# Down-projection one pair later in a software-pipelined mixture-of-experts loop

## What is computed

```
g_sel    = argmax(h @ w_group)                 # one of 8 groups
top_idx  = top_k(e_logits in the group, 2)     # two of its 8 experts
y        = (silu(xb @ w1[e]) * (xb @ w3[e])) @ w2[e]      # for each expert e, xb its tokens
out[tok] += gate * y
```

## Time and profile before

| | |
|---|---|
| median of 3 runs | 1690.52 us |
| lowest, highest | 1689.78, 1690.87 us |
| profiled execution, its own time | 1692.09 us |
| its span in the profile | 1689.8 us |
| mean granted TensorE clock | 0.911 of full speed |
| PE busy | 1341.6 us, 79% |
| DVE, ACT, POOL busy | 480.5, 287.4, 321.6 us |
| read from HBM | 453.15 MB |

### The profile page before, as it was taken

One profiled execution on the slowest core, in us unless ns is written; L12 is line 12 of the kernel. 1 busy time (PEld: TensorE's weight loads), 2 busy tenths in 40 slices (PEclk: granted clock), 3 DMA queues, 4 the chain that ended last, 5 costly groups with the idle time before them and its releaser, 6 DMA issues.

```text
span 1689.8 us, 19504 instructions
## 1 busy us (share of the span) xinstructions
PE 1341.6 (79%) x6100; PEld 630.5 (37%) x6100; DVE 480.5 (28%) x904; ACT 287.4 (17%) x562; POOL 321.6 (19%) x439
## 2 busy tenths in 40 slices
PE   6988984988877878785689699956988787888872
PEld 4555452333332323232444376443333232333330
DVE  6996124111111111111407653142111111111112
ACT  3335110110000001010243433111110000001000
POOL 6303001232222221211000000002232222222210
PEclk9999986999999989998789799977999999999996
DMA  5105541999999999995220302264999999999984
GB/s 204 50 1 219 218 164 62 396 384 406 403 398 403 401 405 410 398 393 218 70 106 1 112 1 103 97 276 169 392 399 399 396 404 398 407 409 395 400 348 178
DMA packets 82068, 464.31 MB, mean 275 GB/s; under 512 B 13457, under 2 KB 15681, under 8 KB 32481
## 3 DMA queue, kind: packets, MB, share of 16 engines
q1 hardware_dynamic: 68640, 436.86, 65.6%
q0 software_dynamic: 11648, 20.47, 3.7%
q10 hardware_dynamic: 1728, 6.29, 0.9%
HBM read 453.15 MB, written 18.94 MB: 279 GB/s over the span
## 4 chain that ended last, share of the span: by engine, by line
PE 41%; SPq 30%; DVE 12%; issue 7%; DMA 6%; ACT 3%; POOLq 0%; POOL 0%; DVEq 0%; ACTq 0%
SPq L1506 20%; PE ps L1368 13%; SPq L1511 10%; PE ps L1388 6%; DMA ring<-in_moe_w 4%; PE ps L442 3%; PE ps L873 2%; PE ps L316 2%; PE ps L431 2%; PE ps L391 2%; DVE ring L541 1%; DMA region_a<-ytok 1%; PE ps L926 1%; DVE extra L541 1%; PE ps L1358 1%
## 5 line engine op out<-in xcount | busy, mean ns | idle before, releaser
L1368 PE MATMUL ps<-ring,region_b 128*64 128x512 f32 x1408 | 344.6, 646 | 76.6 <-issue 57.1
L1368 PEld LDWEIGHTS ps<-ring,region_b 128*64 128x64 f32 x1408 | 117.4, 148 | 301.1 <-issue 270.7
L1368 PE MATMUL ps<-wbuf,region_b 128*64 128x512 f32 x320 | 168.4, 687 | 45.1 <-DMA region_a<-in_moe_w 24.6
L1472 DVE TENSOR_TENSOR extra<-extra,ps 128x256 f32<-128x256 f32 x64 | 26.9, 421 | 614.5 <-ACT extra L1424 574.9
L1388 PE MATMUL ps<-ring,extra 128*64 128x512 f32 x704 | 160.8, 598 | 34.8 <-DVE extra L1478 33.1
L1368 PE MATMUL ps<-region_a,region_b 128*64 128x512 f32 x320 | 168.5, 688 | 0.0
L1312 POOL DMA_INDIRECT region_b<-hrow,icol x128 | 118.6, 926 | 156.1 <-issue 156.1
L1324 POOL DMA_INDIRECT ytok<-extra,icol x128 | 112.2, 877 | 162.6 <-issue 162.6
L1424 ACT ACTIVATE extra<-ps 128x256 f32<-128x256 f32 x64 | 24.5, 383 | 591.6 <-PE ps L1368 583.8
L1485 DVE COPY extra<-ps 128x512 f32<-128x512 f32 x64 | 44.3, 692 | 248.0 <-PE ps L1388 248.0
L1368 PEld LDWEIGHTS ps<-wbuf,region_b 128*64 128x64 f32 x320 | 48.7, 157 | 159.3 <-issue 151.0
(11 more groups left out here) (282 smaller groups left out, 1538.2 us busy)
## 6 DMA issues: line engine op xcount, KB each, us to landing
ring<-in_moe_w SPq DMA_DIRECT2D x264, 1024.0 KB
wbuf<-in_moe_w SPq DMA_DIRECT2D x80, 1024.0 KB
region_a<-in_moe_w SPq DMA_DIRECT2D x40, 1024.0 KB
region_a<-ytok SPq DMA_DIRECT2D x16, 512.0 KB, 5.2
wbuf<-in_ev_w_in SPq DMA_DIRECT2D x3, 2048.0 KB, 17.3
wbuf<-in_ev_w_out SPq DMA_DIRECT2D x2, 2048.0 KB, 14.2
hrow<-region_a ACTq DMA_DIRECT2D x8, 512.0 KB, 9.9
wbuf<-in_mla_w_in SPq DMA_DIRECT2D x2, 1408.0 KB, 25.3
```

The lines of the kernel that those rows point to most:

```text
L1368: last = TE.matmul(ps[CAP * g:CAP * (g + 1), 2 + j, :], xtr[j][:, k, CAP * g:CAP * (g + 1)], up_weights(2 * slot + g, k), start=k == 0, st ...
```

## The change

In each step of the PE list the down-projection of the previous pair now stands between the row transposes of the next pair and the hidden transposes of this pair: up(p), row transposes (p+1), down(p-1), hidden transposes (p). ACT and DVE move their output copies with it; on DVE the output copy (p-1) stands ahead of the hidden copy (p). Pool does gather (p+2), then scatter (p-2). After the last step come one more down-projection, one more output copy and two scatters. SP's list is as it was, and so are all waits inside the stages, the buffers and the slots.

```diff
-            def one(p, n, turn, first=False, last=False):
-                j, slot = n % 2, n % SLOTS
-                te_up(l, p, j, slot, turn, first)
+            def one(i, n, first=False, last=False):
+                p, j = 6 * i + n, n % 2
+                te_up(l, p, j, n % SLOTS, 2 * i + n // SLOTS, first)
                 if not last:
                     te_xtrans(l, p + 1, (j + 1) % 2, False)
+                if not (first and n == 0):
+                    down(i, n - 1, first)
                 te_hidden(l, p, j, first and n == 0)
-                te_down(l, p, j, slot, turn, first and n == 0)
+            def down(i, n, first=False):
+                te_down(l, 6 * i + n, n % 2, n % SLOTS, 2 * i + n // SLOTS, first)
...
+            down(0, NPAIR - 1)
```

```diff
                     gate(p, j, first)
                     if not (last and j == 1):
                         xt(p + 1, (j + 1) % 2, first and j == 0)
-                    yout(p, j, first)
+                    if not (first and j == 0):
+                        yout(p - 1, (j + 1) % 2, first or (second and j == 0))
...
+            yout(NPAIR - 1, 1, False)
```

```diff
                     if not last:
                         ex_gather(l, p + 2, j)
-                    ex_scatter(l, p, j)
+                    if not first:
+                        ex_scatter(l, p - 2, j)
...
+            ex_scatter(l, NPAIR - 2, 0)
+            ex_scatter(l, NPAIR - 1, 1)
```

More of the change, by code:

```diff
@@ L1394, in moe_tensor @@
             te_xtrans(l, 0, 0, True)
-            def one(p, n, turn, first=False, last=False):
-                j, slot = n % 2, n % SLOTS
-                te_up(l, p, j, slot, turn, first)
+            def one(i, n, first=False, last=False):
+                p, j = 6 * i + n, n % 2
+                te_up(l, p, j, n % SLOTS, 2 * i + n // SLOTS, first)
                 if not last:
                     te_xtrans(l, p + 1, (j + 1) % 2, False)
+                if not (first and n == 0):
+                    down(i, n - 1, first)
                 te_hidden(l, p, j, first and n == 0)
-                te_down(l, p, j, slot, turn, first and n == 0)
+            def down(i, n, first=False):
+                te_down(l, 6 * i + n, n % 2, n % SLOTS, 2 * i + n // SLOTS, first)
             for n in range(2):
-                one(n, n, 0, first=True)
+                one(0, n, first=True)
             with TE.Fori(0, 4) as i:
                 for n in range(2, 8):
-                    one(6 * i + n, n, 2 * i + n // SLOTS)
+                    one(i, n)
             for n in range(NPAIR - 6, NPAIR):
-                one(n, n, n // SLOTS, last=n == NPAIR - 1)
+                one(0, n, last=n == NPAIR - 1)
+            down(0, NPAIR - 1)
         def moe_scalar(l):
@@ L1432, in moe_scalar, with two @@
             xt(0, 0, True)
-            def two(i, first, last):
+            def two(i, first=False, last=False, second=False):
                 for j in range(2):
@@ L1439, in two @@
                         xt(p + 1, (j + 1) % 2, first and j == 0)
-                    yout(p, j, first)
[L1441 to L1444, removed]
+                    if not (first and j == 0):
+                        yout(p - 1, (j + 1) % 2, first or (second and j == 0))
+            two(0, True)
+            two(1, second=True)
+            with S.Fori(2, NPAIR // 2 - 1) as i:
+                two(i)
+            two(NPAIR // 2 - 1, last=True)
+            yout(NPAIR - 1, 1, False)
         def moe_gpsimd(l):
@@ L1450, in moe_gpsimd, with two @@
             ex_gather(l, 1, 1, True)
-            def two(i, last):
+            def two(i, first=False, last=False):
                 for j in range(2):
@@ L1456, in two @@
                         ex_gather(l, p + 2, j)
-                    ex_scatter(l, p, j)
-            with G.Fori(0, NPAIR // 2 - 1) as i:
-                two(i, False)
-            two(NPAIR // 2 - 1, True)
+                    if not first:
+                        ex_scatter(l, p - 2, j)
+            two(0, first=True)
+            with G.Fori(1, NPAIR // 2 - 1) as i:
+                two(i)
+            two(NPAIR // 2 - 1, last=True)
+            ex_scatter(l, NPAIR - 2, 0)
+            ex_scatter(l, NPAIR - 1, 1)
         def moe_vector(l):
@@ L1494, in two @@
                         xt(p + 1, (j + 1) % 2, first and j == 0)
+                    if not (first and j == 0):
+                        yout(p - 1, (j + 1) % 2, first or (second and j == 0))
                     hidden(p, j, first)
-                    yout(p, j, first)
[L1497 to L1500, removed]
+            two(0, True)
+            two(1, second=True)
+            with V.Fori(2, NPAIR // 2 - 1) as i:
+                two(i)
+            two(NPAIR // 2 - 1, last=True)
+            yout(NPAIR - 1, 1, False)
         def up_weights_load(b, w, e, s):
```

## The result

The changed kernel takes 1697.28 us (median of 6 runs, 1695.56 to 1703.51) against 1690.69 for the kernel before (median of 6, 1689.08 to 1692.64): 6.6 us more. The ratio, which is that of the mean times, is 1.0045, with a 95% interval from 1.0027 to 1.0063. In a second set of runs it was 1697.65 against 1690.44, 7.2 us more, ratio 1.0050 (1.0037 to 1.0064). By these ratios the loss is 7.6 and 8.5 us, since some runs of the changed kernel are long. The forecast was 1702.1 with a range from 1695.5 to 1709.5. The direction was right and the time lies in the range; the loss is 6.6 to 7.2 us by the medians where the sum said 11.6.

The account below looks back on a forecast made before the run. The prediction took the weight stream to bound most of both expert loops. Start 3.0 plus end 2.8 us, over two layers, gave +11.6 us on 1690.5: 1702.1 us, range 1695.5 to 1709.5.

Parts of the forecast that it names:

- What bounds the kernel: Most of both expert loops: PE waits for weights, stops without a releaser included; removing the 0.76 us wait per step gains 0.
- SP's late release in the middle: Middle steps: SP gets on at 522.7 instead of 516.5 us, but 22 us of transfers are queued, so no cost.
- Rival 2: Leading DMA engines starve because SP gets on late in every step, 8 us a layer: 1718 us; chance 0.08.
- The start, 3.0 us a layer: Start of each layer: pair 3's w2 loads wait for the late down(0), the weight stream stands empty 3.5 us, 3.0 counted.
- Nothing else fills it: Break at the layer start: pair 4's w13 loads stand behind down(0) in SP's list, so the stream stays empty 3.5 us.
- The half microsecond: Deducted from the 3.5 us break: the engine that ends last is still 0.5 us busy when the mean one is empty.
- The end, 2.8 us a layer: End of each layer: down(30) now stands between up(31) and down(31), 15.46 instead of 12.68 us in layer 1.
- the open term: Clock of the last up-projection: 7.09 us taken after 1.4 us idle; the slow case would add 1.7 us in layer 1.
- rival 1: The lagging DMA engine carries the stream over the break, only the ends cost, 5.6 us: 1696 us; chance 0.12.
- Rival 3: Stops without a releaser are PE's own; some 15 steps save 0.76 us each, 11.4 in all: 1680 us; chance 0.05.
- Rival 4: No effect: PE's shorter step and an absorbed break leave under 3.4 us; chance 0.05.
- The signs: Forecast wrong if up(31) of either layer starts earlier than before, or the DMA share in the middle drops below 1.

Follow-up runs that it names:

- mid: Changed kernel with both ends in the old order: down-projections late only from pair 3 on, down(30) ahead of up(31); ratio 1.0007 to the kernel before.
- later: Kernel before, with SP from pair 6 on also waiting for down(p-2) before it loads w2 of pair p; ratio 0.9999.
- head2: Kernel before, with only down(0) moved behind up(1) and the row transposes of pair 2, and Pool in the new order; 1694.26 us, ratio 1.0024.
- tailold: Changed kernel with down(30) put back ahead of up(31); 1694.8 us, ratio 1.0031 to the kernel before.
- hole: Kernel before, with SP waiting for down(1) instead of down(0) before it loads w2 of pair 3; 1705.38 us, ratio 1.0085.
- warm: Changed kernel with SP's list shifted too, plus six unused float32 matmuls ahead of up(31); 1687.62 us, ratio 0.9981 to the kernel before.
- pool: Kernel before with Pool's list alone in the new order: gather (p+2), then scatter (p-2); ratio 0.9995.
- head: Kernel before, with only down(0) moved behind up(1) and the row transposes of pair 2, Pool's list old; 1698.62 us, ratio 1.0053.

## Why the prediction was right or wrong

**What bounds the kernel: right.** The claim was that a wait removed in front of a weight wait only lengthens the latter. By mid the middle of the change costs 0.0007 of the time (-0.0002 to 0.0016), with the reserve on its last step said there, and in the changed kernel the idle time went from the down-projections to the up-projections.

**SP's late release in the middle: right.** I had 22 us of transfers queued when SP gets on. Later delays the release by about as much as the change, at no cost. Rival 2, leading DMA engines that starve, is out with later and mid; it had 8 in 100.

**The start, 3.0 us a layer: the right place, the wrong size.** "Nothing else fills it" is the step that failed. The time between the two issues was forecast within 0.13 us. But I took the weight traffic before the break at 423 GB/s and the break as empty. In the changed kernel the gathers of pairs 3 and 4 fall into these 14 us. With them the first weights run at 384 GB/s, and part of their traffic is served in the break itself; that it is then missing from the full stream later is inferred. Left is 1.4 to 1.8 us of idle engines a layer, and a delay of up(31) of 1.2 us in the mean. By the times the break is dearer: head2 against before and tailold against mid both give 4.1 us for the two layers, 2 a layer. Both ways it is less than 3.0. With Pool's old list the idle time is 2.8 us. Part by part I had set down that Pool's order costs and gives nothing; alone that is so, beside the break it is worth some 2 us a layer. The half microsecond that I deducted for a lagging engine was no more than a guess in the right direction: hole passed nearly all of its 7.2 us on.

**The end, 2.8 us a layer: right, 2.6.** 12.69 to 15.29 us where the last up ran at full clock before and after, and 14.39 to 16.99 where it was slow in both. That the last up-projection is still weight-bound was right as well: it idled for 0.84 to 3.73 us. Its clock was the open term: with 1.4 us of idle time I took the fast case; in one profile it idled 3.40 and 3.73 and was slow in both layers, in the other 1.18 and 0.84 and fast in both. In layer 0 the sum took it for slow in both kernels; in the second profile it was not, and that layer's end was only 0.9 us longer than before.

**The sum.** By the measured terms 2 x (1.2 + 2.6) = 7.6 us, or 9.2 with 2 us a layer for the break, against 6.6 and 7.2 by the medians and 7.6 and 8.5 by the ratios. The forecast of 11.6 was 1.6 to 1.8 times too large by the medians, nearly all of it from the break, since the end was off by only 0.2 us a layer. That the time still lies in the range is owed to a low end that was drawn to take in rival 1, not to the size of the break. Rival 1 (the break is absorbed, 1696) came nearer in its number and was wrong in its mechanism: a lagging engine does not carry the stream over a hole. **Rival 3** (PE paces the last steps, faster) is refuted by mid and by the time: without the wait of the down-projection nothing got faster, and 54.8 us more of waiting appeared at the up-projections. That the stops without a releaser are weight waits too was argued and is not shown in the trace, since the growth went to the stops on a named transfer. **Rival 4** is out.

**The signs.** One of the two signs of being wrong came up by its letter: in the first profile up(31) of layer 0 started 0.04 us earlier than before. That is far inside what two profiles of one kernel differ by, 1.8 us here, so the sign was too sharp for one profile. The other did not: the DMA share in the middle is 1.01.

What stays open: why up(30) started up to 2 us earlier in mid, and how far single profiles of one kernel scatter in these starts; two profiles of the changed kernel differ by 1.8 us.

## What to carry to other kernels

When one step of a pipelined loop moves, look up who else waits for it in a list of its own: here SP's list held four loads back that were free to go, and the repair was to shift that list too, which turned a loss of 0.5% into a gain of 0.2%. In a loop that waits for a stream, removing waits inside the step buys nothing; look at where the stream starts, where it breaks, and at how much work stands behind its last transfer. Price a break by the time in which the DMA engines have nothing to do, with all other queues' traffic in the sum, and not by the gap between two loads.

## What the runs showed of the hardware

- A float32 matmul with 128 columns of weights and 512 of data left two records, 0.44 us apart: twelve records and 5.32 us for six instructions in warm. A price taken from the spacing of such records has to be doubled. With 64 columns of weights there is one record each: 32 records in 7.09 us for the 32 matmuls of an up-projection.
- The last up-projection of a layer followed the idle time before it: 7.04 to 7.09 us after up to 1.18 us idle, 8.68 to 8.78 after 2.31 to 3.73, 9.46 after 5.28 and 9.93 after 5.02. The order is not strict: elsewhere in the loop of the kernel before one took 10.06 us after 3.26 idle.
- Small indirect transfers, issued while the weight queue is full, are not free: with a pair's gathers in the stretch the engines stayed full at 384 (changed) and 399 GB/s (pool) instead of 423 (before) and 422 (head).
